# A two-block transformer kernel: attention visits in two half-steps, five score banks, first-norm squares on ScalarE, and a mixer whose small matmuls come three tiles at a time

## The reference, cut to what matters

```python
G = jnp.cumsum(lfc, axis=2)
o_inter = jnp.einsum('bhtk,bhkv->bhtv', qc * jnp.exp(G), S)
diff = G[:, :, :, None, :] - G[:, :, None, :, :]
decay = jnp.where(mask, jnp.exp(jnp.minimum(diff, 0.0)), 0.0)
scores = jnp.einsum('bhtk,bhsk,bhtsk->bhts', qc, kc, decay)
```

## Time and profile before

| | us |
|---|---|
| median of 3 runs | 1276.0 (1275.64 to 1281.35) |
| the profiled execution's own time | 1279.9 |
| its span, first to last instruction | 1278.1 |
| TensorE busy in the span | 1234.3 |
| mean granted TensorE clock | 0.987 of full speed |

### The profile page before, as it was taken

One profiled execution on the slowest core, in us unless ns is written; L12 is line 12 of the kernel. 1 busy time (PEld: TensorE's weight loads), 2 busy tenths in 40 slices (PEclk: granted clock), 3 DMA queues, 4 the chain that ended last, 5 costly groups with the idle time before them and its releaser, 6 DMA issues.

```text
span 1278.1 us, 17097 instructions
## 1 busy us (share of the span) xinstructions
PE 1234.3 (97%) x6230; PEld 982.5 (77%) x6230; DVE 658.9 (52%) x1217; ACT 550.4 (43%) x1066; POOL 659.0 (52%) x501
## 2 busy tenths in 40 slices
PE   7998989999999999999989999999999999999996
PEld 5886767777878888888776676878888888888885
DVE  6436744765743312125277545459999999200024
ACT  4544544676654333235552647542332333322344
POOL 4772223235346544446454464646767776655542
PEclk9998999999999999999988999999999999999998
DMA  5333222113222433343231121423333333433321
GB/s 197 112 113 98 67 61 73 50 50 83 67 66 83 114 92 91 95 152 112 82 84 50 42 71 53 116 82 84 99 99 99 90 92 87 128 96 94 100 74 66
DMA packets 63939, 113.94 MB, mean 89 GB/s; under 512 B 7016, under 2 KB 12776, under 8 KB 63856
## 3 DMA queue, kind: packets, MB, share of 16 engines
q1 hardware_dynamic: 63712, 112.84, 31.0%
q10 hardware_dynamic: 144, 0.00, 0.0%
HBM read 110.71 MB, written 2.11 MB: 88 GB/s over the span
## 4 chain that ended last, share of the span: by engine, by line
PE 83%; DVE 9%; ACT 3%; issue 2%; POOL 1%; DMA 1%; DVEq 0%; SPq 0%; ACTq 0%; POOLq 0%
PE pb L911 24%; PE pb L912 24%; PE pb L914 24%; PE pb L1065 2%; PE pb L1041 1%; DVE P L1774 1%; PE pb L1016 1%; POOL HL L2191 1%; DVE B L1644 1%; PE pb L979 1%; DVE U L1644 1%; DVE sq L1632 1%; PE pb L981 1%; PE pb L980 1%; POOL wlo L2191 1%
## 5 line engine op out<-in xcount | busy, mean ns | idle before, releaser
L2191 POOL TENSOR_TENSOR wlo<-raw,whi 128x512 fp32r<-128x512 f32 (+3 forms) x398 | 539.6, 1372 | 437.7 <-ACT whi L1247 437.5
L911 PE MATMUL pb<-HH,whi 128*128 128x512 f32 x968 | 391.4, 404 | 0.0
L912 PE MATMUL pb<-HL,whi 128*128 128x512 f32 x968 | 384.1, 397 | 0.0
L914 PE MATMUL pb<-HH,wlo 128*128 128x512 f32 x968 | 382.6, 395 | 0.0
L1247 ACT ACTIVATE whi<-raw 128x512 fp32r<-128x512 f32 (+3 forms) x398 | 233.2, 613 | 184.5 <-PE pb L914 156.5
L911 PEld LDWEIGHTS pb<-HH,whi 128*128 128x128 f32 x968 | 183.3, 189 | 47.0 <-issue 3.7
L914 PEld LDWEIGHTS pb<-HH,wlo 128*128 128x128 f32 x968 | 182.7, 189 | 42.6
L912 PEld LDWEIGHTS pb<-HL,whi 128*128 128x128 f32 x968 | 182.9, 189 | 42.2 <-issue 2.4
L1644 DVE SCALAR_TENSOR_TENSOR cv<-zf,vecs,cv 128x512 f32<-128x512 f32 x88 | 124.9, 1419 | 3.1
L1322 ACT ACTIVATE P<-P,stat 128x256 f32<-128x256 f32 (+3 forms) x96 | 51.1, 533 | 92.9 <-DVE stat L1639 68.9
L1635 DVE TENSOR_TENSOR X<-pb,X 128x512 f32<-128x512 f32 x24 | 16.6, 691 | 137.7 <-PE pb L914 137.3
(11 more groups left out here) (386 smaller groups left out, 1913.1 us busy)
## 6 DMA issues: line engine op xcount, KB each, us to landing
raw<-in_wall SPq DMA_DIRECT2D x362, 256.0 KB, 2.7
raw<-in_wall SPq DMA_DIRECT2D x16, 192.0 KB, 2.4
raw<-in_wall SPq DMA_DIRECT2D x8, 260.0 KB, 3.1
X<-in_xT SPq DMA_DIRECT2D x8, 256.0 KB, 5.3
N<-c_sums SPq DMA_DIRECT2D x8, 256.0 KB, 4.1
X<-in_xT SPq DMA_DIRECT2D x2, 1024.0 KB, 7.7
outT<-PP SPq DMA_DIRECT2D x8, 256.0 KB, 2.2
raw<-in_wall SPq DMA_DIRECT2D x12, 128.0 KB, 2.1
```

The source lines that it names most:

```text
L911: pe.do.matmul(b, hi, xh[k], start=start, stop=False)
L912: pe.do.matmul(b, hi, xl[k], start=False, stop=False)
L914: m = pe.do.matmul(b, lo, xh[k], start=False, stop=stop)
L2191: g.do.tensor_tensor(lo, x, hi.bitcast(F32), ALU.subtract).then_inc(*up(name, point))
```

## The change

Attention: the visit now has two yields. The first issues scores, values, transposes and the normalisation of the first group; the second, half a tile later, normalises the second group and prepares the next. `slot` advances at i == 3 and i == 7, `kA` tile 1 has no slot, and `vA` steps at every k. Score banks are 4, 5, 6, 3, 2; the projection ring in the background stage is banks 0 and 1.

```diff
-        self.held, self.score_banks = {}, (4, 5, 6)
+        self.held, self.kept, self.clock, self.score_banks = {}, {}, 0, (4, 5, 6)
...
-        banks = {"main": (0, 1, 2, 3), "first3": (0, 1, 2), "S": (), ...
+        banks = {"main": (0, 1, 2, 3), "first2": (0, 1), "S": (), ...
...
     def slot(self, i):
-        if i == 7:
+        if i in (3, 7):
             self.step()
...
         for i in range(0, n + 6, 2):
             two = groups[i:i + 2]
-            if 0 < i <= n:
-                for u in groups[i - 1]:
-                    self.add("normal", *u)
...
-            for g in groups[i + 2:i + 4]:
-                for u in g:
-                    self.add("pre", *u)
...
             yield
+            if two:
+                for u in two[1]:
+                    self.add("normal", *u)
+                for g in groups[i + 2:i + 4]:
+                    for u in g:
+                        self.add("pre", *u)
+                yield
...
-        self.score_banks = (4, 5, 6, 3)
+        self.score_banks = (4, 5, 6, 3, 2)
         for name in ("kA", "qA"):
             for t in range(4):
-                self.tile("first3", (name, t), between=None if (name, t) == ("kA", 0) else self.slot)
+                self.tile("first2", (name, t), between=None if name == "kA" and t < 2 else self.slot)
```

```diff
-        add("lambda")
...
         add("columns1")
+        add("lambda")
...
             add("vC", k)
-            add("x_norm", k)
+            if k % 2 == 0:
+                add("x_norm", k // 2)
...
         def sums(i):
+            if i % 2 == 0:
+                add("x_norm", 4 + i // 2)
...
                 a.do.activation(mh[k], xk[k], ACT.Copy, scale=vecs("norm_gain", k)).then_inc(*up("xhi", ("m_hi", k)))
+                if k > 2:
+                    a.wait_ge(*at("sq_step", k - 2))
+                a.do.activation(sqs[(k - 1) % 2] if k else acc, xk[k], ACT.Square).then_inc(*up("a_norm", ("sq", k)))
```

```diff
-    def tick(self, i=1):
-        if i % 2:
-            self.ticks += 1
-            if self.ticks % 2:
-                self.advance(self.gates)
+    def tick(self, i=None):
+        if i in (1, 5, None):
+            self.advance(self.gates)
+        if i in (3, 7, None):
             self.advance(self.heads)
...
+        add("decays")
+        add("logs")
+        add("base_far")
         for t in range(3):
-            self.tile("x5", ("bq", t), "win2")
+            tile("bq", t)
             if t == 0:
...
                 add("columns2")
+                add("log_sums")
             add("bq_out", t)
...
+            if t:
+                add("level", 4, t - 1)
+            add("query", t)
+            if t == 0:
+                add("inverse")
+        add("level", 4, 2)
```

Head norms: tiles now come in the order `cb`, `bg`, `ag`. Heads 3 and 4, 5 and 6, and 7 are summed during `cb` and `bg`. `wout` starts with five tiles over heads 3, 4, 5, 6; meanwhile heads 0, 1, 2 follow one another, with a step after every block k:

```diff
+        def last_norms():
+            for _ in range(4):
+                yield
+            for t in range(3):
+                add("square_a", t)
+                yield
+                take(("head", t))
+                add("head_sums", t)
+                yield
+                add("head_out", t)
+
+        self.heads.append(last_norms())
+        for d in range(NFIRST):
+            take(("wout", d), keep=True)
+            self.proj(("wout", d), "wout", P * d, WK[:4], stop=False, between=lambda i: tick())
...
+            def square_a(t):
+                if t == 0:
+                    tables(LNEXP)
```

More of the change, by code:

```diff
@@ L168, in take, with take_any, release @@
         self.hold(banks[n % len(banks)], tile)
+    def take_any(self, tile, keep=False):
+        bank = min((b for b in range(8) if b not in self.kept), key=lambda b: self.held.get(b, -1))
+        self.hold(bank, tile)
+        if keep:
+            self.kept[bank] = tile
+    def release(self, tile):
+        del self.kept[self.bank[tile]]
+        self.clock += 1
+        self.held[self.bank[tile]] = self.clock
     def hold(self, bank, tile):
@@ L172, in hold @@
         self.before[tile] = self.holder.get(bank)
-        self.held[bank] = len(self.bank)
+        self.clock += 1
+        self.held[bank] = self.clock
         self.holder[bank] = tile
@@ L359, in gate @@
                 self.step()
[L360 removed]
+            self.tile("first2", (name, t), between=self.slot)
             add("gate_out", name, t)
         def gm(d, j):
[L364 removed]
+            take("first2" if self.background else "main", ("gm", d, j))
             self.proj(("gm", d, j), "win", GM + 1024 * j + P * d, between=self.slot)
@@ L483, in norm_steps @@
             yield
[L484 to L491 removed]
+            yield from self.head_norms([[3, 4], [5, 6], [], [7]])
         self.heads.append(norm_steps())
         for t in range(2):
[L495 to L504 removed]
+            tile_out("cb", t, tick)
+        for t in range(3):
+            tile_out("bg", t, tick)
+            while self.heads:
+                tick()
+            if t:
+                add("head_out", 2 + t)
+            residual()
+        for t in range(3):
+            tile("ag", t)
+            if t == 0:
+                add("head_out", 5)
+                residual()
+            add("ag_out", t)
+            release(("ag", t))
+        def last_norms():
+            for _ in range(4):
+                yield
+            for t in range(3):
+                add("square_a", t)
[5 more added lines that the diff above has]
+        self.heads.append(last_norms())
+        for d in range(NFIRST):
+            take(("wout", d), keep=True)
+            self.proj(("wout", d), "wout", P * d, WK[:4], stop=False, between=lambda i: tick())
         while self.heads:
@@ L526, in second @@
         for d in range(8):
-            take("all", ("down", d))
+            take(("down", d))
             self.proj(("down", d), "ffn_dn", P * d, range(NPAIR))
@@ L530, in second @@
         for d in range(8):
-            take("all", ("pp", d))
+            take(("pp", d))
             self.proj(("pp", d), "ple_p", P * d, range(2))
@@ L534, in second @@
         for d in range(6):
-            take("all", ("pg", d, 0))
+            take(("pg", d, 0))
             self.proj(("pg", d, 0), "ple_g", P * d)
@@ L542, in half_tile @@
         def half_tile(half, d):
-            take("all", ("pg", d, half))
+            take(("pg", d, half))
             add("half_tile", half, d)
@@ L549, in second @@
         half_tile(1, 6)
-        take("all", ("norm4", 0))
+        take(("norm4", 0))
         add("half_out", 0)
```

278 lines of the change are left out of this document (136 added, 142 removed).

## The result

The changed kernel took 1286.3 us (median of 6 runs, 1284.6 to 1287.3), the kernel before 1279.6 in the same series (6 runs, 1275.6 to 1281.4): a ratio of 1.0059, with a 95% interval of 1.0042 to 1.0076. It is slower by 0.6%, where 1262 and "faster" had been forecast. Against the 1279.6 of this series the forecast sum of -14.2 would have been 1265.4; what came is +6.7. The profiled execution took 1287.1 us for a span of 1285.3.

The account below looks back on a forecast made before the run. TensorE, busy 1234.3 of 1278.1 us, was taken as the bound, so only its idle, slow-clock and switching time could go. The terms summed to -14.2, taking 1276.0 to 1261.8, stated as 1262, range 1246 to 1272.

Parts of the forecast that it names:

- First norm: Start of the kernel: moving `lambda` and the squares to ScalarE ends TensorE's idle time, slow clock and late split; -4.5 us.
- `kA` 0: First `kA` tile: a new wait for the bank of `qC` 2, freed late behind x_norm 6 and 7; +2 us (0 to +4).
- Visits for C: Attention visits for C: a fifth score bank shortens transpose waits; -1.6 us at the second visit, -2 between 115 and 165 us.
- In `vA`: Seventh visit for C, moved into `vA` with three banks: fourth score tile and transposes wait one step longer; +1.2 us.
- Visits for A: Attention visits for A: with the second group normalised half a tile earlier, all but one step of waiting goes; -3.5 us.
- `bq`, `bv`, levels and switches: Wait at `bv` 2.5 instead of 4.6, level waits and clock gone, 25 visits become 12; -9.8 us together.
- The new waits at the levels: Levels 8 to 32 in `bv`: with three tiles at once the third waits for the first's merge; +1 us (0 to +4).
- Head norms: Last head norms: each head a chain of 3.8 us, giving TensorE waits of 1.9, 1.4 and 1.4; +4 us net.
- The waits cost clock too: Rival: waits at the norms and `kA` 0 also lower the clock, and `bv` stays as before; 1269 us, chance 0.17.
- the ring of two banks: Rival: with two projection banks, some 35 background tiles each wait 0.7 us for late evacuation; +24, 1286 us, chance 0.08.
- the sentence on the table load: Head norms: the skill's 2.66 us per table switch, against 1.28 traced, would lengthen the first wait by 1.4, giving 1263.

## Why the prediction was wrong

The forecast missed by 24.3 us (1286.3 against 1262). 3.6 of them are not the change's: 1276.0 was the median of three executions, and six of the same kernel gave 1279.6. Against that the sum of -14.2 missed by 20.9, since +6.7 came.

Four alterations, each timed by itself, bring 7.4 (order of the visits), 7.2 (last norms), 5.4 (bias rows) and 4.3 (`x_norm`), 24.3 in all, and together 23.1. So most of the lost time lies at these four places, and it can be had back. That their sum is the miss to the tenth is luck: the early bias rows remove a stall that the kernel before had too and that the forecast had left in, and the nine steps ahead of the last norms are more than was there before. Term by term the four places missed by 22.0 (the table), and that is argued from one trace of each kernel.

- **First norm, -4.5: right in kind, too small at its place, too large at the end.** The idle time for `lambda` and the slow clock went, the matmul by ones starts at 29.89 where 31 was forecast, and 5.6 us are won by the end of `kC`. But I had taken for granted that a gain of TensorE stays. `x_norm` in `vC` goes at GpSimd's pace, one low part of x and one of the weights, 2.95 us for each k; that was hidden by TensorE's being late. By itself the part brings 3.6 us behind `vC` and 2.4 (0.5 to 3.6) in the time.
- **`kA` 0, +2: the mechanism was there, mis-sized.** The step that failed is "x_norm 6 holds the chain of forget sums back by about 0.9". `x_norm` 6 began only at 71.74, since it needs a buffer that GpSimd's low part of `x_norm` 4 reads until 71.7, and took 1.77 us beside GpSimd, though the trace of before has `x_norm` at 1.76 to 1.79 us in `vC`; with the low part behind it the chain, whose matmuls were done at 71.4, began at 74.04, 2.6 us late. So the scan was late too, for which no wait had been forecast. It came to 3.3 us of waits and, with slow clock from 80.8 to 87.6, to +5.9.
- **Visits for C, -1.6 and -2: the step on the second visit failed.** "The first transpose no longer waits, the second waits" was right as to the order, but the sum is the same: VectorE is as late as before, and the one wait left is 3.75 instead of 3.00 and 0.87. I had found the cause, the DMA that is issued with the visit, and did not follow it. With the rows early, 5.4 us come. In `vA`, put at +1.2, the waits from 155 to 180 us are 5.5 instead of 3.8, and the clock fell there, which it had not before (0.66 in 165 to 170 us).
- **Visits for A, -3.5, and the start of B, at nothing: the step that failed most.** "Evacuations of projection tiles now come after exps begun half a tile before, not after a visit just begun" holds only while visits fall in the middle of a tile. Each pipeline has 19 steps, an odd number, and B's follows A's directly, so that its visits fall at the end of a tile, and the gate's tanh comes behind the exps. I did not count the steps. But the place in the tile is not the whole cause: half a tile later the start of B gave back 1.1 us, a whole tile later 2.8, and whole-tile visits, which stand at a tile's end too, have no wait there. I had not asked what VectorE has to do between two visits when a last norm, a gate tile and a second group meet: there the wait is 5.4 us, and with its clock it is 7.1. That the half-tile order brings it is shown, by whole-tile visits; the share of each of these causes is argued from the timeline. For A the mechanism was right but the size was not: the transposes' waits from 200 to 292 us are 3.5 us before, 1.5 in the changed kernel, and 3.5 again with whole-tile visits and five banks. So the early normalisation is worth 2.0 of the 3.5, and over all of the time up to 286 us the order is worth about 1 us.
- **`bq`, `bv`, levels and switches, -9.8: -8.5, close, and in part by luck.** One wait of 2.5 was forecast at `bv`; it is 1.5 and 0.6. The new waits at the levels were put at +1, within 0 to 4, and are 4.1. That the slow clock of 655 to 660 and 695 to 700 is gone makes up for much of it: the first had been forecast to stay, and the second was put at 2 us from one window, though the one before it, 690 to 695, has 0.71 too, and it cost about 3.2; a new one, 0.66 in 670 to 675, is behind the longest of the new waits, 2.1 us.
- **Head norms, +4: mechanism right, mis-sized.** Waits of 1.9, 1.4 and 1.4 were forecast and are 3.0, 2.1 and 1.0, as the head's chain is 4.6 us and not 3.8. To that come 1.9 at an earlier sum, and the step "fewer than 2 us idle at a time; the clock I leave alone" was wrong: the clock was at half from 801.0 to 807.8 (0.60 and 0.72 in the two windows), where about 2.9 us of work are lost, and 1.6 are in 750 to 755 (0.68). In all +12.0.
- **The rivals.** "The waits cost clock too" named the direction and two of the places, at 1269, and missed B. The slower one, the ring of two banks, did not happen: but for one wait of 1.3 us at `vA` and that of 1.4 at `kA` 0, which went when `x_norm` moved, TensorE waits for no evacuated projection bank in 80 to 360 us. That it named 1286, the measured time, is chance. What happened was an adding up of stalls at four places. (In the sentence on the table load the 1261.5 should be the sum's 1261.8; nothing hangs on it.)

Left open: why 2.1 us of wait stay at the start of B when it comes a tile later and the cast is gone, while whole-tile visits leave none. The backlog of low parts on GpSimd is there (5 us in one piece) and VectorE's operations beside it are long, but no run took that backlog away.

## What to carry to other kernels

When an order of steps is changed, look at the joints first, and count the steps to find where they fall: the last steps of one, the first of the next and whatever else falls between them have to fit into one engine's queue, and a mean over many visits says nothing of that. A chain whose stages run on three engines in turn wants its stages for several items side by side (all squares, then all sums), and its first consumer placed behind the time that the chain needs. And where TensorE is made earlier, ask which engine had only just kept up with it.

## What was not expected of the hardware

VectorE and GpSimd hold each other up in whole operations. In the run with B a tile later an addition on 128x1 took 1.15 and 1.26 us beside GpSimd and 0.15 without it, and a scaling of 128x128 1.10; a reciprocal between them (0.16) and the score operation, which reads one of TensorE's banks (0.28 at 293.50), were not lengthened. In the changed kernel a multiply by the norm took 1.77 beside GpSimd, and 0.74 without. The Trainium skill ("SBUF — State Buffer", section "SBUF: two separate sides") says that the two share a pair of ports under an exclusive lock, which a VectorE operation with two inputs in SBUF, or one in a two-port mode, asks for, and that the later one stands until the other's instruction ends. By that rule a short operation costs up to one GpSimd operation, here 1.25 to 1.3 us, however small it is (an estimate); the traces agree for the additions and the multiply. The scaling has one tensor as input; whether it was in a two-port mode no run here shows.

The same wait brought the clock down in one execution and not in another. Three lines show it (windows as above). The first two are the run with `x_norm` wholly as before and that with the first norm alone; both have one wait of 2.4 us for the `vC` banks, which ends just before 70 us, and no other wait near it. The third is the run with `x_norm` 4 to 7 behind `vC`, at the last norms:

```profile
70.00:75.00 5.00, 5.00 (x16) 3.96 (x17) 0.00 (x0) 3.41 (x9) 3.68 (x3) 0.69 0.26 78
...
70.00:75.00 5.00, 5.00 (x27) 3.66 (x26) 0.68 (x1) 2.50 (x6) 3.92 (x4) 1.00 0.30 77
...
790.00:795.00 5.00, 4.06 (x9) 2.40 (x10) 0.75 (x1) 2.47 (x4) 1.36 (x2) 0.66 0.34 98
```

There the clock fell (from 2.4 to 1.2 GHz) right behind the first wait of 2.98 us, which ended at 789.97, and before the second; with the squares together the same first wait left it at 1.00. In the changed kernel it fell at 80.8 behind a single wait of 1.91, and in 670 to 675 behind one of 2.1; with the squares together a wait of 2.1 us at the same place left it at 1.00. So a wait of about 2 to 3 us costs nothing more, or up to some 3 us of work lost at half clock. What decides it no run here shows, and one trace does not tell whether an alteration saved the clock. The medians over several executions hold both cases, and that is a reason not to read differences of 1 us between them.
